# mLSTM in chunked form: masked scores only inside each 128-token tile, carried key-value states between tiles in both directions

## The reference

```python
def mlstm_scan(q, k, v, li, lf):          # chunks of 64 tokens, one direction
    def step(carry, inp):
        C, n, m = carry
        b = jnp.cumsum(lfc, axis=-1)
        dmat = jnp.where(tril, b[..., :, None] - b[..., None, :] + lic[..., None, :], NEG)
        m_inter = b + m[..., None]
        m_t = jnp.maximum(m_inter, dmat.max(axis=-1))
        w = jnp.exp(dmat - m_t[..., None]) * jnp.einsum('bhtd,bhsd->bhts', qc, kc)
        s_inter = jnp.exp(m_inter - m_t)
        num = s_inter[..., None] * jnp.einsum('bhtd,bhdv->bhtv', qc, C) + jnp.einsum('bhts,bhsv->bhtv', w, vc)
        den = s_inter * jnp.einsum('bhtd,bhd->bht', qc, n) + w.sum(axis=-1)
        h = num / jnp.maximum(jnp.abs(den), jnp.exp(-m_t))[..., None]
        ...
h = mlstm_scan(forward) + flip(mlstm_scan(flip of all))
```

## Time and profile before

| | us |
|---|---|
| median of 3 runs | 1765.33 (1765.05 to 1765.89) |
| span of the profiled execution | 1767.8 |
| busy TensorE, VectorE, ScalarE, GpSimd in it | 1653.6, 602.6, 218.1, 269.1 |
| mLSTM stage, from the q projection of pair 0 to the start of attention | 51.8 to 292.9 |
| mean granted TensorE clock | 0.974 |

### The profile page before, as it was taken

The page is one execution under the profiler, slowest core; times in us unless marked ns, Lnnn a source line. Parts: engine busy times, 40 slices in busy tenths (PEclk is TensorE's granted clock), DMA queues, the critical chain, the costliest instruction groups (busy, mean ns, idle before and its releaser), DMA issues.

```text
span 1767.8 us, 32445 instructions
## 1 busy us (share of the span) xinstructions
PE 1653.6 (94%) x13879; PEld 783.0 (44%) x13879; DVE 602.6 (34%) x1051; ACT 218.1 (12%) x466; POOL 269.1 (15%) x342
## 2 busy tenths in 40 slices
PE   7999999999999999899989898999989998999976
PEld 5666675554554445434333333333333333433324
DVE  4554556543452113561312213122122231312225
ACT  2312221221230001100000000000000000000001
POOL 2010011000004001412121211212112112121101
PEclk9999999999999999899999899999999999999989
DMA  6332332211115314499999999999999999999996
GB/s 200 118 102 70 119 122 55 63 39 50 36 26 159 95 55 207 158 365 409 428 420 418 424 409 426 395 428 425 422 406 422 430 422 412 414 422 421 412 428 281
DMA packets 97115, 491.11 MB, mean 278 GB/s; under 512 B 12320, under 2 KB 65808, under 8 KB 79280
## 3 DMA queue, kind: packets, MB, share of 16 engines
q1 hardware_dynamic: 83152, 458.28, 64.5%
q0 software_dynamic: 12528, 30.53, 5.0%
q10 hardware_dynamic: 1312, 0.42, 0.1%
HBM read 470.67 MB, written 23.76 MB: 280 GB/s over the span
## 4 chain that ended last, share of the span: by engine, by line
PE 71%; DMA 25%; DVE 2%; issue 2%; ACT 0%; POOL 0%; SPq 0%; ACTq 0%; POOLq 0%; DVEq 0%
PE PS L1963 24%; DMA ring<-in_w 23%; PE PS L456 22%; PE PS L1975 7%; PE PS L1784 6%; PE PS L1872 3%; PE PS L1746 2%; PE PS L1827 2%; DMA ring<-y_dram 1%; PE PS L1698 1%; PE PS L1831 1%; PE PS L1817 1%; PE PS L1635 1%; DMA x_sb<-in_x 0%; PE PS L2048 0%
## 5 line engine op out<-in xcount | busy, mean ns | idle before, releaser
L1963 PE MATMUL PS<-ring,mix_sb 128*32 128x512 f32 x5376 | 616.1, 617 | 60.5 <-DMA ring<-in_w 60.4
L1963 PEld LDWEIGHTS PS<-ring,mix_sb 128*32 128x32 f32 x5376 | 173.9, 114 | 485.0 <-issue 397.5
L1975 PE MATMUL PS<-ring,hm_sb 128*32 128x256 f32 x5376 | 296.3, 379 | 0.8 <-DMA ring<-in_w 0.8
L1529 DVE TENSOR_TENSOR low_sb<-PS,low_sb 128x1536 f32<-128x1536 f32 (+1 forms) x32 | 49.9, 1558 | 609.6 <-PE PS L1963 609.6
L1975 PEld LDWEIGHTS PS<-ring,hm_sb 128*32 128x32 f32 x5376 | 172.5, 110 | 132.1 <-issue 19.0
L456 PE MATMUL PS<-uT_sb,ring 128*128 128x512 f32 (+3 forms) x400 | 141.9, 511 | 0.0
L1022 ACT ACTIVATE hm_sb<-hm_sb 128x768 f32<-128x768 f32 (+1 forms) x32 | 24.5, 766 | 714.8 <-DVE hm_sb L1531 714.8
L821 POOL COPY ints<-ints 128x3 int32 (+1 forms) x30 | 5.6, 185 | 679.1 <-ACT hm_sb L1028 679.1
L456 PEld LDWEIGHTS PS<-uT_sb,ring 128*128 128x128 f32 x400 | 75.4, 190 | 64.3 <-issue 59.3
L766 POOL DMA_INDIRECT mix_sb<-xt_dram,ints x84 | 86.5, 1030 | 64.9 <-POOL ints L808 22.2
L792 POOL DMA_INDIRECT y_dram<-hm_sb,ints x80 | 80.4, 1005 | 43.5 <-POOL ints L821 24.5
(11 more groups left out here) (319 smaller groups left out, 1299.1 us busy)
## 6 DMA issues: line engine op xcount, KB each, us to landing
ring<-in_w SPq DMA_DIRECT2D x58, 4096.0 KB, 20.3
ring<-in_w SPq DMA_DIRECT2D x72, 2048.0 KB, 14.7
ring<-in_w_in SPq DMA_DIRECT2D x24, 512.0 KB, 4.0
ring<-in_w_in SPq DMA_DIRECT2D x8, 1024.0 KB, 5.4
y_dram<-at_sb POOLq DMA_DIRECT2D x4, 2048.0 KB, 10.6
ring<-in_w SPq DMA_DIRECT2D x8, 1024.0 KB, 4.7
ring<-y_dram SPq DMA_DIRECT2D x4, 2048.0 KB, 23.5
ring<-m_dram POOLq DMA_DIRECT2D x16, 256.0 KB, 5.0
```

Source lines behind the costliest of these rows:

```text
L1529: V.tensor_tensor(hid, PS[:, at:at + g, :], b1_row.unsqueeze(1).broadcast_to([P, g, 2 * QR]), ALU.add).then_inc(hid_used, 1)
L1963: last = nc.tensor.matmul(PS[32 * j:32 * j + 32, at + t, :].rearrange("p (c n) -> p c n", c=2), xgT[n][:, k, 32 * t:32 * t + 32], w1_c[k][ ...
L1975: last = nc.tensor.matmul(PS[32 * j:32 * j + 32, Y_BANK + t, 0:QR], actT[:, k, 32 * t:32 * t + 32], w2_in[k // 2][:, k % 2, j * QR:(j + 1) ...
```

## The change

Inside a pair the scores and decays are kept only for the diagonal tiles (128 queries against the same 128 keys). Everything farther away comes from a state, a 64 by 129 matrix for each head, direction and tile: keys times their decay to the tile's edge (`k_in`, `k_meta`) multiplied with values (`grown`), added up from tile to tile with a factor (`grow`), and read by queries times their own decay (`q_in`).

This needs keys with tokens on the partitions (`turn_k`: 5 transposes of `kT`), decays of the keys as columns (`ak_col`, built in the prelude and turned with the gates), and decays of the queries as rows (`qs_nat`, exponentiated in the prelude, stored to a second DRAM tensor `q_dram`, spread to 64 partitions for each head and direction by four more DMAs into `q_fall`).

```diff
@@ GpSimd
-        pool.wait_ge(m_stored, 16)
+        pool.wait_ge(rows_stored, 32)
         def norms(i):
             for hh in range(2):
                 for d in range(2):
                     src = m_dram[bass.ds(i * 2 + (32 * d + hh), 1), :]
                     pool.dma_start(m_bc[:, hh, d, :], src.partition_broadcast(P)).then_inc(ml_m, 16)
+            for hh in range(2):
+                for d in range(2):
+                    src = q_dram[bass.ds(i * 2 + (32 * d + hh), 1), :]
+                    pool.dma_start(q_fall[DQK * hh:DQK * hh + DQK, d, :], src.partition_broadcast(DQK)).then_inc(ml_m, 16)
             clear_plane(i)
+            pool.wait_ge(ml_m, i * 128 + 128)
+            pool.wait_ge(q_ready, i + 1)
+            for d in range(2):
+                nc.gpsimd.tensor_tensor(q_in[:, d, :], qT, q_fall[:, d, :], ALU.mult).then_inc(q_in_ready, 1)
@@ ScalarE, prelude (ahead of the square root of L890)
+        act.wait_ge(exp_in, 3)
+        st.alone(nc.scalar.activation(qs_nat[0:64, META:TK], qs_nat[0:64, META:TK], ACT.Exp))
+        act.dma_start(q_dram[:, :], qs_nat[0:64, META:TK]).then_inc(rows_stored, 16)
+        act.wait_ge(exp_in, 4)
+        st.alone(nc.scalar.activation(ak_rep[0:H, :], ak_rep[0:H, :], ACT.Exp))
+        nc.scalar.activation(ak_nat[0:64, :], ak_nat[0:64, :], ACT.Exp).then_inc(exp_out, 1)
@@ ScalarE, ml_pair
             for hh in range(2):
                 act.wait_ge(diag_ready, i * 16 + (8 * hh + 8))
-                (7 exponentials of off-diagonal and meta tiles)
-                st.did(nc.scalar.activation(diagonal(hh, 0), diagonal(hh, 0), ACT.Exp))
-                nc.scalar.activation(diagonal(hh, 1), diagonal(hh, 1), ACT.Exp).then_inc(decay_ready, 1)
+                for d in range(2):
+                    nc.scalar.activation(diagonal(hh, d), diagonal(hh, d), ACT.Exp).then_inc(decay_ready, 1)
@@ VectorE, prelude
         dve.sem_inc(gates_ready, 1)
+        st.did(nc.vector.memset(qs_nat[32:64, META + (MT - 1) * P:TK], 0.0))
+        st.did(nc.vector.tensor_tensor(by_tile(qs_nat, 0, slice(0, MT)), ..., ALU.subtract))
+        st.did(nc.vector.tensor_tensor(by_tile(qs_nat, 32, slice(0, MT - 1)), ..., ALU.subtract))
+        st.settle()
+        dve.sem_inc(exp_in, 1)
         natural(a_nat, a_row)
         st.settle()
-        st.did(nc.vector.tensor_copy(a_rep[0:64, :]...))
+        (memset, tensor_scalar, a copy and two tensor_tensor for ak_nat and ak_rep)
+        st.settle()
+        dve.sem_inc(exp_in, 1)
@@ VectorE, ml_pair
+            st.did(nc.vector.tensor_copy(ak_pair[:, 0:MT], ak_by[:, 0:MT, :, bass.ds(i * 2, 2)]))
+            st.did(nc.vector.tensor_copy(ak_pair[:, MT, 0], ak_by[:, MT, 0, bass.ds(i * 2, 2)]))
             st.settle()
-            dve.wait_ge(ml_m, i * 64 + 64)
+            dve.wait_ge(ml_m, i * 128 + 128)
             (16 operations on diagonal tiles, kT copies, gated: as before)
+            dve.wait_ge(pe_k, i * 2 + 2)
+            (3 tensor_tensor: k_in forwards, k_in backwards, k_meta, from PSUM).then_inc(k_ready, 1)
             dve.wait_ge(pe_v, i + 1)
             (copies of v: as before)
-            (18 products of scores and decays, in five steps)
+            for hh in range(2):
+                dve.wait_ge(decay_ready, i * 4 + (2 * hh + 2))
+                dve.wait_ge(pe_s, i * 3 + (hh + 1))
+                st.did(nc.vector.tensor_tensor(diagonal(hh, 0), bank(hh), diagonal(hh, 0), ALU.mult))
+                nc.vector.tensor_tensor(diagonal(hh, 1), bank(hh), diagonal(hh, 1), ALU.mult).then_inc(s_used, 1)
+            dve.wait_ge(pe_s, i * 3 + 3)
+            (2 copies and 5 scalar_tensor_tensor: the states).then_inc(s_used, 1)
@@ TensorE
+        def turn_k():
+            for j in range(MT):
+                nc.tensor.transpose(PS[:, 1, j * P:(j + 1) * P], kT[:, j * P:(j + 1) * P], ident)
+            nc.tensor.transpose(PS[:, 2, 0:P], kT[:, T:T + P], ident).then_inc(pe_k, 1)
+
+        def scores():
+            for j in range(MT):
+                for hh in range(2):
+                    h0, c = DQK * hh, slice(j * P, (j + 1) * P)
+                    last = nc.tensor.matmul(PS[:, hh, c], kT[h0:h0 + DQK, c], qT[h0:h0 + DQK, c], start=True, stop=True)
+                    if j == MT - 1:
+                        last.then_inc(pe_s, 1)
+
+        def grown():
+            for d, j in ((0, MT), (0, 0), (0, 1), (0, 2), (1, 3), (1, 2), (1, 1)):
+                for hh in range(2):
+                    (out: 64 partitions, those of the head; w: 128 by 64; v: 129 columns)
+                    last = nc.tensor.matmul(out[h0:h0 + DQK], w, v, start=True, stop=True)
+            last.then_inc(pe_s, 1)
@@ TensorE, ml_pair (behind turn_h or turn_gates, ahead of the v projection)
+            pe.wait_ge(k_ready, i * 2 + 1)
+            turn_k()
             pe.wait_ge(ml_w[1], i * 16 + 16)
             (v projection: as before)
-            pe.wait_ge(k_ready, i + 1)
+            pe.wait_ge(k_ready, i * 2 + 2)
             (meta rows of v: as before)
-            scores(i, 0), output gate 1, scores(i, 1 to 3), output gate 2 with scores(i, 4) inside
+            scores(), output gate 1, grown(), output gate 2
+            pe.wait_ge(q_in_ready, i * 2 + 2)
+            pe.wait_ge(s_used, i * 3 + 3)
             for hh in range(2):
                 for m in range(MT):
-                    fwd = [(dec_f(hh, j)[:, c], v_sb[:, j, hh, :]) for j in range(m + 1)] + [(dec_f(hh, MT)[:, c], v_sb[:, MT, hh, :])]
-                    bwd = [(dec_b(hh, j)[:, c], v_sb[:, j, hh, :]) for j in range(m, MT)]
+                    fwd = [(q_in[h, 0, c], state_f[m][h]), (diagonal(hh, 0)[:, c], v_sb[:, m, hh, :])]
+                    bwd = [(diagonal(hh, 1)[:, c], v_sb[:, m, hh, :])]
+                    if m < MT - 1:
+                        bwd = [(q_in[h, 1, c], state_b[m][h])] + bwd
```

More of the change, by code:

```diff
@@ L240, in build @@
     m_dram = dram("m_dram", [64, T], F32)
+    q_dram = dram("q_dram", [64, T], F32)
     dve_steps, act_steps, pool_steps = sem("dve_steps"), sem("act_steps"), sem("pool_steps")
@@ L354, in build @@
     wv_s, wo_s = view(ring, slot(1), KT, 2 * DV), view(ring, slot(2), KT, 2 * DV)
[L355 to L361, removed]
-    def diagonal(hh, d):
-        at = slot(3) + hh * DEC + d * 5 * T
-        return view(ring, at, MT, T + P)[:, :, 0:P]
+    def diagonal(hh, d):
+        return view(ring, slot(3) + (2 * hh + d) * T, T)
+    q_fall, q_in = view(ring, slot(4), 2, T), view(ring, slot(4) + 2 * T, 2, T)
+    k_in = [view(ring, slot(5) + d * T, MT, 2, DQK) for d in range(2)]
+    k_meta = view(ring, slot(5) + 2 * T, 2, DQK)
+    STATE = DV + 2
+    state_f = [view(ring, slot(6) + n * STATE, DV + 1) for n in range(MT)]
+    state_b = [view(ring, slot(6) + (MT + n) * STATE, DV + 1) for n in range(MT - 1)]
+    grown_f = [PS[:, 3 + n // 3, (n % 3) * (DV + 1):(n % 3 + 1) * (DV + 1)] for n in range(MT)]
+    grown_b = [PS[:, 2, 0:DV + 1], PS[:, 4, 2 * (DV + 1):3 * (DV + 1)], PS[:, 4, DV + 1:2 * (DV + 1)]]
     m_bc = view(ring, slot(8), 2, 2, T)
@@ L510, in _ @@
             load_ml(i, True)
-        sp.wait_ge(pe_k, PAIRS)
+        sp.wait_ge(pe_k, 2 * PAIRS - 1)
         def load_at(i, again):
@@ L528, in _ @@
         load_at(0, False)
-        sp.wait_ge(decay_ready, 2 * PAIRS)
+        sp.wait_ge(s_used, 3 * PAIRS)
         sp.dma_start(rope_q, c_rope[:, :, 0:T]).then_inc(rope_in, 16)
@@ L1156, in natural, with by_tile, at_tile @@
             st.did(nc.vector.tensor_copy(nat[32:64, META:TK], row[32:64, 0:T][:, ::-1]))
+        def by_tile(t, p0, tiles):
+            return t[p0:p0 + 32, META + P * tiles.start:META + P * tiles.stop].rearrange("p (a b) -> p a b", b=P)
+        def at_tile(t, p0, first, n):
+            return t[p0:p0 + 32, first:first + (n - 1) * P + 1][:, ::P].unsqueeze(2).broadcast_to([32, n, P])
         natural(nm_nat, top_row)
@@ L1222, in ml_pair, with grow @@
             nc.vector.tensor_copy(v_sb[:, MT, :, 0:DV], PS[:, 2, 256:512].rearrange("p (b c) -> p b c", b=2)).then_inc(v_ready, 1)
[L1224 to L1235, removed]
+            for hh in range(2):
[3 more added lines that the diff above has]
+                nc.vector.tensor_tensor(diagonal(hh, 1), bank(hh), diagonal(hh, 1), ALU.mult).then_inc(s_used, 1)
+            def grow(new, old, fall, grown):
+                return nc.vector.scalar_tensor_tensor(new, old, fall, grown, ALU.mult, ALU.add)
+            dve.wait_ge(pe_s, i * 3 + 3)
+            st.did(nc.vector.tensor_copy(state_f[0], grown_f[0]))
+            st.did(nc.vector.tensor_copy(state_b[MT - 2], grown_b[MT - 2]))
+            st.settle()
+            for n in range(1, MT - 1):
+                st.did(grow(state_f[n], state_f[n - 1], q_fall[:, 0, n * P - 1:n * P], grown_f[n]))
+                m = MT - 2 - n
+                st.did(grow(state_b[m], state_b[m + 1], q_fall[:, 1, (m + 1) * P:(m + 1) * P + 1], grown_b[m]))
+                st.settle()
```

(21 more changed lines are left out.)

71 lines of the change are left out of this document (37 added, 34 removed).

## The result

The changed kernel takes 1811.61 us (median of 4 runs, 1810.57 to 1814.80) against 1765.43: a ratio of 1.0263, 95% interval 1.0249 to 1.0277. It is slower by 46 us; 1806 was forecast, with 1786 to 1820 as the range. The profiled execution spans 1811.0 us where the one before spanned 1767.8.

The account below looks back on a forecast made before the run. TensorE was taken to bound the stage that changes (71% of the chain, 25% DMA). Prelude and pair 0 +18.2, pairs 1 to 3 +22.2: +40.4 us on the 1767.8 span, 1808.2, less 2.5: 1806, range 1786 to 1820.

Parts of the forecast that it names:

- The wait for `kT`: Ahead of `turn_k`, before the v projection: TensorE waits 7.6 us in pairs 1 to 3, about 12 in pair 0.
- The new DMAs: GpSimd issues eight DMAs instead of four, so the rows VectorE waits for land 2.6 us later (2.0 to 3.5).
- The clock: TensorE's granted clock falls behind the longer waits, in prelude and every pair; loss 2.0 us each (1.0 to 3.0).
- The prelude: ScalarE's square root comes behind the new exponentials: TensorE waits 4.8 us longer (3.5 to 5.5), plus 2.0 for the clock.
- Scores and `grown`: TensorE, each pair: scores fall from 4.90 to 1.3 us (0.9 to 2.0); the new `grown` adds 1.9.
- the change of form: Going into and out of the form where two heads run at once on TensorE costs about 0.2 us, whatever the count.
- PV: TensorE, each pair's end: 60 records instead of 96 take 9.5 us (6.7 to 9.9) instead of 10.72.
- an excursion: In PV, a 64-row product standing between full ones: 14 in all, at 0.2 us each 2.8.
- the gain of 2.9 for each pair: TensorE from v projection to pair's end: 41.84 us instead of 44.76, before added waits and clock loss.
- Sum: Whole kernel: pair 0 with prelude +18.2 and pairs 1 to 3 +22.2 make +40.4 us.
- The 2.5 taken off at the end: Last step: the profiled span of 1808.2 us, less its 2.5 over the median, gives the predicted time of 1806.

Follow-up runs that it names:

- the run that parts them: Against the changed kernel (1811.6 us), the four new DMAs signal their own semaphore, so the diagonal tiles wait for the first four alone: 1808.04 us.
- Filled waits: Against the changed kernel (1811.6 us), matmuls whose result nobody reads ahead of the wait for kT, 12 in pair 0, 7 in the others: 1802.15 us.
- the grouped run: Against the changed kernel (1811.6 us), PV's seven 64-row products in each head stand together ahead of the eight full ones: 1793.46 us.

## Why the prediction was right, point by point

- **The wait for `kT`.** Predicted 7.6 us in pairs 1 to 3, measured 7.10, 6.78 and 6.97; in pair 0 about 12, measured 11.92. The diagonal tiles started 16.9 us into the pair where 17.3 was forecast. Moving the transposes gave back 39.9.
- **The new DMAs.** 2.6 later predicted; 2.2 measured by the two kernels' starts of the diagonal tiles (16.9 against 14.7), 1.8 to 2.4 by the run that parts them.
- **The clock.** Predicted 2.0 at each of five places, 10 in all. Its row is of the experts: behind 3.65 us of idle time the same 192 records took 2.53 longer, with the granted clock at 0.50 for the first 5 us of them. That the longer waits here would do the same was an inference from this one place; the runs bear it out. Filled waits gave back 8.8 for four, and the rope matmuls behind the fifth take 1.8 longer: 10.6.
- **The prelude.** Predicted + 6.8 up to the start of pair 0's q projection; it starts at 58.67 instead of 51.78, + 6.9.
- **Scores and `grown`.** 1.3 and 1.9 predicted, 1.09 and 1.70 measured. Both run two at once: one after the other would be 1.8 and 3.1, at once 0.9 and 1.6. For weight loads that a short matmul can't hide, the trace before has a case at 678.89: 16 records of 32 columns took 1.70 us, 0.106 each where 0.441 for 512 columns makes 0.028, and weights of 128 by 128 were being loaded during all of the 1.70. The scores' 0.2 above 0.9 leaves nothing for it beside the 0.2 of the change of form.
- **The term that was mis-sized: PV.** "At 0.2 each that is 2.8: 9.5 (6.7 to 9.9)". Measured 12.05, outside these bounds, because an excursion of one 64-row product among full ones costs 0.38, not 0.2. The 0.2 was taken from runs of two heads at once, and carried over to a single product without a row for it. Why a single one costs more, no run shows. That the cost falls due at each of the 14 was the author's estimate, and the runs agree: the 60 records take 12.05 us with 14 excursions, 7.39 with 2 and 6.79 with none. The shortfall is 4 x 2.55 = 10.2 us, and it turned the gain of 2.9 for each pair, from the v projection on, into 0.9 (13.91 + 1.00 + 1.09 + 7.06 + 1.70 + 7.06 + 12.05 = 43.87 against 44.76, with v at full clock).
- **Sum.** The mLSTM stage and prelude were forecast 40.4 longer and are 47.3: 10.2 more for PV, 3.3 less for the rest, mainly the smaller scores, `grown` and waits. So the misses partly cancel, and that is luck. The stage is 6.9 over its forecast; outside it the medians (46.2 apart) leave 1.1 less, within what executions differ there, and so the total is 5.6 over the 1806.
- **The 2.5 taken off at the end.** The prediction compares a span with a time. The time is 1.6 above the span of the same execution (1812.59 and 1811.0), so the profiled execution before, with its span of 1767.8, was not 2.5 but about 4 us above the median. It does no harm here, since 40.4 on the median of 1765.3 gives the same 1806.

## What to carry to other kernels

When a consumer moves ahead in one engine's order, everything that stands ahead of its producer in the producer's order begins to count: look up when the producer's result was ready in the old trace, and what stands ahead of it there, needed or not. Here k was 4.9 us late for the new place before the change added anything, and of the 46 us one moved loop of transposes gives back 40, or three copies put ahead of a DMA wait 30.

When products of half the rows are mixed with full ones, put them side by side, or pad them to all rows: here 30 products took 12.05 us in alternating forms, 7.39 side by side and 6.79 padded, where 48 of one form had taken 10.72.

## What the runs showed of the hardware

A 64-row product alone among 128-row ones costs 0.38 us more than its place in line (12.05 against 6.79 us for the same 60 records, 14 excursions). A product padded to 128 rows with zeros takes 0.113 us for a record, where the 96 of PV before took 0.112 each.

Behind waits of 4.7 to 11.9 us, as behind the 3.65 of the earlier trace rows, TensorE's work ran at a granted clock of 0.50, and 1.00 came back 2.8 to 6.0 us after it resumed. The two ends, each in 2 us stretches: resumed at 152.13 behind an idle of 6.69 (pair 1 of the grouped run), and at 288.29 behind an idle of 5.36 (pair 3 of the run with the new DMAs apart):

```profile
152.13:154.13 2.00, 2.00 (x8) 0.50 0.75 187
154.13:156.13 2.00, 2.00 (x9) 0.81 0.02 4
...
292.29:294.29 2.00, 2.00 (x6) 0.50 0.00 0
294.29:296.29 2.00, 2.00 (x11) 1.00 0.00 0
```

So the same kind of wait cost between 0.8 and 2.4 us in the v projection behind it. With the waits filled down to 0.5 to 1.4 us the v projections took 13.91, as with the granted clock at 1.00 throughout. A transpose's record is 0.27 us long with the granted clock at 1.00 (pair 1 with the waits filled) and 0.42 with it at 0.50 (pair 1 of the changed kernel).
